# Expert tiles with the first half's activation transposes inside the second half's gate/up matmuls, ScalarE and VectorE in another order, and GpSimd computing 3 of 12 low parts

## The reference

```
for e in range(16):
    hid = silu(xt @ W_gate_e[e]) * (xt @ W_up_e[e])     # 1024 -> 512, twice
    y = y + combine[:, e:e+1] * (hid @ W_down_e[e])     # 512 -> 1024
```

## Time and profile before

| | |
|---|---|
| median of three runs | 1472.57 us |
| the profiled execution, span of its page | 1482.0 us |
| expert stage in it | 903 to 1414 us |
| PE busy over the span | 1236.9 us (83%) |
| DVE, ACT, POOL busy | 848.6, 639.1, 219.0 us |

### The profile page before, as it was taken

How to read it: one execution, slowest core, us unless ns; L and a number is a source line. 1 busy time by engine, 2 the same in 40 slices (tenths; PEclk the granted TensorE clock), 3 DMA queues, 4 the chain that set the end, 5 groups by cost and what they waited for, 6 DMA issues and landing times. The chain is left out here.

```text
span 1482.0 us, 24876 instructions
## 1 busy us (share of the span) xinstructions
PE 1236.9 (83%) x7835; PEld 1011.2 (68%) x7836; DVE 848.6 (57%) x1812; ACT 639.1 (43%) x1250; POOL 219.0 (15%) x307
## 2 busy tenths in 40 slices
PE   6479998999899999999589972999899989899910
PEld 1178876988697868887368752777677777777800
DVE  2623773367426762377445766587754575557339
ACT  4333453345434453345412214476543464446224
POOL 0200320022102220032000112011011101011132
PEclk9789998999899998999699985999899999999965
DMA  7513122221222122320453325889966596866156
GB/s 281 159 43 90 51 58 60 78 58 56 60 67 71 54 58 57 88 79 15 139 148 127 118 70 191 304 288 313 321 210 204 189 320 202 276 226 226 58 182 214
DMA packets 201385, 215.29 MB, mean 145 GB/s; under 512 B 15368, under 2 KB 166464, under 8 KB 201024
## 3 DMA queue, kind: packets, MB, share of 16 engines
q1 hardware_dynamic: 179136, 174.40, 37.1%
q0 software_dynamic: 10064, 34.42, 6.5%
q10 hardware_dynamic: 12112, 5.41, 1.3%
HBM read 187.40 MB, written 26.79 MB: 145 GB/s over the span
## 5 line engine op out<-in xcount | busy, mean ns | idle before, releaser
L703 PE MATMUL mixers_ps_proj<-early_h_hi,mixers_w_hi 128*128 128x352 f32 x384 | 129.5, 337 | 33.2 <-POOL mixers_a_hg L482 27.6
L1735 PE MATMUL experts_ps_g<-experts_w_hi,experts_x_hi 128*128 128x512 f32 x384 | 150.7, 392 | 2.2 <-DVE experts_x_lo L1664 2.2
L1736 PE MATMUL experts_ps_g<-experts_w_lo,experts_x_hi 128*128 128x512 f32 x384 | 150.4, 392 | 0.0
L1737 PE MATMUL experts_ps_g<-experts_w_hi,experts_x_lo 128*128 128x512 f32 x384 | 150.3, 391 | 0.0
L495 POOL TENSOR_TENSOR mixers_k_lv<-mixers_decay,mixers_hk 128x1024 f32<-128x1024 f32 (+2 forms) x40 | 79.7, 1995 | 343.1 <-ACT mixers_decay L571 333.2
L1659 DVE TENSOR_TENSOR experts_w_lo<-all_raw,experts_w_hi 128x1024 fp32r<-128x1024 f32 x96 | 113.8, 1223 | 27.5 <-ACT experts_w_hi L1608 24.5
L729 PE MATMUL mixers_ps_proj<-mixers_w_hi,early_h_hi 128*128 128x512 f32 (+1 forms) x288 | 119.8, 416 | 9.9 <-DVE mixers_w_lo L851 9.9
L704 PE MATMUL mixers_ps_proj<-early_h_lo,mixers_w_hi 128*128 128x352 f32 x384 | 127.3, 332 | 0.0
L705 PE MATMUL mixers_ps_proj<-early_h_hi,mixers_w_lo 128*128 128x352 f32 x384 | 127.2, 331 | 0.0
L1659 DVE TENSOR_TENSOR experts_w_lo<-experts_raw_more,experts_w_hi 128x1024 fp32r<-128x1024 f32 x96 | 111.8, 1221 | 14.4 <-ACT experts_w_hi L1608 13.1
L731 PE MATMUL mixers_ps_proj<-mixers_w_hi,early_h_lo 128*128 128x512 f32 (+1 forms) x288 | 114.0, 396 | 0.0
(11 more groups left out here) (269 smaller groups left out, 2710.9 us busy)
## 6 DMA issues: line engine op xcount, KB each, us to landing
experts_raw_more<-in_W_down_e_dram SPq DMA_DIRECT2D x128, 256.0 KB, 5.1
all_raw<-in_W_gate_e_dram SPq DMA_DIRECT2D x96, 256.0 KB, 5.7
all_raw<-in_W_up_e_dram SPq DMA_DIRECT2D x96, 256.0 KB, 6.7
all_raw<-in_W_in_dram SPq DMA_DIRECT2D x32, 512.0 KB, 4.2
all_raw<-in_W_ada_dram SPq DMA_DIRECT2D x32, 512.0 KB, 4.0
y_scratch<-experts_y POOLq DMA_DIRECT2D x24, 512.0 KB, 4.4
condition_w_ada_in<-in_W_ada_dram SPq DMA_DIRECT2D x4, 2048.0 KB, 8.2
experts_raw_more<-in_W_gate_e_dram SPq DMA_DIRECT2D x32, 256.0 KB, 3.5
```

The source lines that it names most:

```text
L703: pe.matmul(out, whi, xhi, start=(k == 0), stop=False)
L1735: pe.matmul(out, x_hi[:, k, :], w_hi[:, c, at], start=(k == 0), stop=False)
L1736: pe.matmul(out, x_hi[:, k, :], w_lo[:, c, at], start=False, stop=False)
L1737: ins = pe.matmul(out, x_lo[:, k, :], w_hi[:, c, at], start=False, stop=(k == KD - 1))
```

## The change

TensorE issues `turn_h(0)` in the middle of the second half's gate/up, after chunk 5, and `turn_h(1)` after the first quarter of the down projection. ScalarE and VectorE work on the turned hidden activation and on the chunks in an order to match. The low parts of chunks 2, 6 and 10 are computed by GpSimd in place of VectorE, with a semaphore of their own; in a tile that carries a split GpSimd does chunks 2 and 6 before its gather, and chunk 10 between the gather and the store of `y`.

```diff
+POOL_CHUNKS = (2, 6, 10)
@@ sync
-                    sp.wait_ge(lo_done, sp.snap(x * CH + (c + 1 - CH)))
+                    sp.wait_ge(*lo_count(sp, sp.snap(x - 1), c))
@@ gpsimd
+            def split(x, c, first):
+                pool.wait_ge(hi_done, c + 1 if first else pool.snap(x * CH + (c + 1)))
+                if not first:
+                    carry(pool, idle)
+                pool.tensor_tensor(w_lo[:, c], raw[c], f32(w_hi[:, c]), ALU.subtract).then_inc(pool_lo, 1)
+
+            for c in POOL_CHUNKS:
+                split(0, c, True)
+
             def tile(x, t, j, last, last_expert):
+                splits = last and not last_expert
+                following = pool.snap(x + 1) if splits else None
+                if splits:
+                    split(following, POOL_CHUNKS[0], False)
+                    split(following, POOL_CHUNKS[1], False)
                 start = pool.value_load(s.plan[0:1, bass.ds(x, 1)], min_val=0, max_val=SLOTS)
...
                 pool.wait_ge(xt_done, pool.snap(t + 1))
                 carry(pool, idle)
                 gather(column, pool.snap(t + 2))
+                if splits:
+                    split(following, POOL_CHUNKS[2], False)
                 pool.wait_ge(y_stored, pool.snap(t * 16 + 16))
@@ scalar (vector alike: product, h_low and x_low; its split skips POOL_CHUNKS)
                 some(0, 3)
                 silu(0)
-                some(3, 6)
+                some(3, 5)
+                h_high(0)
+                some(5, 7)
                 silu(1)
-                h_high(0)
+                h_high(1)
                 x_high(t)
-                h_high(1)
-                some(6, 9)
+                some(7, 11)
                 act.wait_ge(used, act.snap(t * CH + CH))
                 act.wait_ge(y_stored, act.snap(t * 16 + 16))
                 act.activation(y[:, 0:512], ps_y[0][:, :], ACT.Copy).then_inc(y0_done, 1)
-                some(9, CH)
+                some(11, CH)
@@ tensor
                         c = 4 * half + k // 2
+                        if half == 1 and k == 4:
+                            turn_h(0)
...
-                turn_h(0)
                 turn_x(t)
-                turn_h(1)
                 pe.wait_ge(y0_done, pe.snap(t + PRIMED))
                 pe.wait_ge(y1_done, pe.snap(t + PRIMED))
                 for f in range(KF):
+                    if f == 1:
+                        turn_h(1)
```

More of the change, by code:

```diff
@@ L1520, in phase_experts @@
         lists_in, index_done = sem("lists_in"), sem("index_done")
-        hi_done, lo_done, used = sem("hi_done"), sem("lo_done"), sem("used")
+        hi_done, used = sem("hi_done"), sem("used")
+        dve_lo, pool_lo = sem("dve_lo_done"), sem("pool_lo_done")
         x_in, xt_done, xhi_done, xlo_done = sem("x_in"), sem("xt_done"), sem("xhi_done"), sem("xlo_done")
@@ L1528, in phase_experts, with lo_count @@
         ident = s.const("ident")
+        def lo_count(e, x, c):
+            by_pool = c in POOL_CHUNKS
+            n = len(POOL_CHUNKS) if by_pool else CH - len(POOL_CHUNKS)
+            nth = 1 + sum((k in POOL_CHUNKS) == by_pool for k in range(c))
+            at = x * n + nth if isinstance(x, int) else e.snap(x * n + nth)
+            return (pool_lo if by_pool else dve_lo), at
         def experts(e, tile):
@@ L1657, in split @@
             def split(x, c, first):
+                if c in POOL_CHUNKS:
+                    return
                 dve.wait_ge(hi_done, c + 1 if first else dve.snap(x * CH + (c + 1)))
-                dve.tensor_tensor(w_lo[:, c], raw[c], f32(w_hi[:, c]), ALU.subtract).then_inc(lo_done, 1)
+                dve.tensor_tensor(w_lo[:, c], raw[c], f32(w_hi[:, c]), ALU.subtract).then_inc(dve_lo, 1)
             def x_low(t):
@@ L1689, in tile @@
                 product(0)
-                some(3, 6)
+                some(3, 5)
+                h_low(0)
+                some(5, 7)
                 product(1)
-                h_low(0)
+                h_low(1)
                 x_low(t)
-                h_low(1)
-                some(6, 9)
+                some(7, 11)
                 dve.wait_ge(used, dve.snap(t * CH + CH))
@@ L1724, in tile, with turn_h @@
                 t2 = pe.snap(t * 2 + PRIMED)
-                chunk0 = pe.snap(x * CH) if not isinstance(x, int) else x * CH
                 pe.wait_ge(xlo_done, pe.snap(t + 1))
                 pe.wait_ge(hid_done, t2)
+                def turn_h(n):
+                    pe.wait_ge(hid_done, pe.snap(t2 + (n + 1)))
+                    pe.wait_ge(hlo_done, t2)
+                    for f in range(2):
+                        ins = pe.transpose(ps_h[n][:, f, :], hid[:, (2 * n + f) * P:(2 * n + f + 1) * P], ident)
+                    ins.then_inc(ht_done, 1)
                 for half in range(2):
@@ L1739, in tile @@
                             ins.then_inc(used, 1)
-                def turn_h(n):
-                    pe.wait_ge(hid_done, pe.snap(t2 + (n + 1)))
-                    pe.wait_ge(hlo_done, t2)
-                    for f in range(2):
-                        ins = pe.transpose(ps_h[n][:, f, :], hid[:, (2 * n + f) * P:(2 * n + f + 1) * P], ident)
-                    ins.then_inc(ht_done, 1)
-                turn_h(0)
                 turn_x(t)
-                turn_h(1)
                 pe.wait_ge(y0_done, pe.snap(t + PRIMED))
```

4 lines of the change are left out of this document (2 added, 2 removed).

## The result

| | median of runs | range | ratio to before, 95% interval |
|---|---|---|---|
| before | 1471.73 us | 1469.38 to 1473.05 (4 runs) | |
| changed kernel | 1637.03 us | 1632.14 to 1639.94 (4 runs) | 1.111 [1.107, 1.1151] |

The changed kernel is slower by 165 us. The forecast was 1622 us, with 1560 to 1690 around it. The profiled execution of the changed kernel has a span of 1630.5 us. For before there are two profiled executions: that of the rows ahead of the prediction (1482.0 us) and a second one, taken later (1467.1 us, at a time of 1468.78 us). Where they differ I give both.

A forecast was written before the change was run, and what follows sets the result against it. The prediction took the late gather, queued on GpSimd, as what TensorE waits for. Terms 47.6 (singles) + 77 (closing tiles) + 13 (tile 0) + 12 (extras) = 149.6 us on the 1472.57 median gave 1622 us, range 1560 to 1690.

The forecast's parts named there:

- The mechanism: GpSimd's queue: gather held behind chunk 6's low part, issued at T0+15.6 in place of T0+4.7; split tiles take 29.6 us.
- The closing tiles: Seven closing tiles carrying a split: each grows from 18.6 to 29.6 us by the late gather, +77 us.
- The singles: Seven singles after tile 0: each grows from 22.8 to 29.6 us by the late gather, +47.6 us.
- tile 0: First tile of the stage, 21.8 us before: gather about 5 us later than in the template, +13 us.
- The extras: Eight extras: store of y and gather 2.4 us later, thinner traffic against it; +1.5 each, 12 us (bounds -1, +4 each).
- The signs: Traces expected: turn_x waits some 9 us in 15 tiles, late gather, idle weight queue, y store at T0+4, clock near 0.5.
- The longer chain: Split tiles: same held gather with every step at its upper bound, 34.7 us a tile, +248 us, 1720; chance 0.08.
- the shorter: Split tiles: same held gather with every step at its lower bound, 24.9 us a tile, +56 us, 1529; chance 0.08.
- Blocking without a held gather: 15 tiles: VectorE and GpSimd only block each other, up to 2.4 us each, at most 36 us, 1509; chance 0.02.
- The faster rival: GpSimd's waits for chunks 2 and 6 met by T0+1.8, only TensorE's saved waits remain: about -5 us, 1467; chance 0.01.
- The rule of the Trainium skill: VectorE two-SBUF-input and GpSimd SBUF-reading instructions exclude each other, up to 2.4 us per chunk; sum said to be unchanged.

The follow-up runs named there:

- Experiment 4: Changed kernel with all 12 low parts on VectorE; GpSimd only waits for chunk 6's high part ahead of the gather, no arithmetic: 1626.6 us, against 1508.73 without the wait.
- experiment 1: Changed kernel with GpSimd's plan load and gather moved ahead of all three of its low parts: 1478.2 us, ratio 1.0043.
- Experiment 9: Changed kernel with chunk 2's low part given back to VectorE; chunks 6 and 10 stay on GpSimd where they stand: 1621.05 us, ratio 1.0989.
- experiment 2: Changed kernel with all 12 low parts back on VectorE, keeping the new places of turn_h and the new engine order: 1508.73 us, ratio 1.0256.
- experiment 3: Changed kernel with GpSimd's chunks 2, 4, 10 in place of 2, 6, 10: 1612.85 us, ratio 1.0953.

## Why the prediction was right, step by step

**The mechanism** was named and holds. Experiment 4 shows the wait by itself, experiment 1 takes it away. The steps of a tile that carries a split (us after T0):

| | forecast | closing tile at 1202.61 | single at 1281.86 |
|---|---|---|---|
| high part of chunk 6 ends | 11.3 | 11.0 | 12.7 |
| low part of chunk 6 ends | 13.7 | 13.8 | 15.6 |
| gather issued | 15.6 | 14.8 | 16.6 |
| `turn_x` starts | 20.6 | 20.9 | 23.9 |
| next gate/up starts | 29.6 | 29.2 | 32.1 |

For the closing tiles each step is within 1 us. Two errors cancel: the gather was issued 0.8 us sooner than forecast, because plan and index cost 1.0 us behind the low part and not 1.9, and it landed in 6.1 us and not in 5.0. The estimate of 5.0 took the queues as empty from T0+13.8 on; the loads issued until T0+14.9 were still in flight (DMA share 0.84 over the wait).

**The singles** were mis-sized, by 2.5 us each. Their mean: gather issued at T0+16.7 and not 15.6, landing 6.7 us and not 5.0, 8.7 us behind `turn_x` and not 9.0. The landing is the largest of the three, and the closing tiles have it too (6.3 us). The late issue is the singles' own, and a step of the mechanism failed there: the prediction costed VectorE's slower subtractions at nothing, since "VectorE is not waited for". In the single at 1281.86, VectorE, GpSimd and TensorE in this order:

```profile
1286.64 4.57 DVE L1689 TENSOR_TENSOR experts_w_lo<-all_raw,experts_w_hi 128x1024 fp32r<-128x1024 f32 x2
1291.13 0.41 DVE L1710 TENSOR_TENSOR experts_hid<-experts_act_g,experts_ps_g 128x256 f32<-128x256 f32 x1
```

```profile
1287.38 2.73 POOL L1595 TENSOR_TENSOR experts_w_lo<-all_raw,experts_w_hi 128x1024 fp32r<-128x1024 f32 x1 [1.23 <-ACT experts_w_hi L1635]
```

```profile
1291.59 0.44 PE L1763 MATMUL experts_ps_h<-all_consts_sb,experts_hid 128*128 128x128 f32 x2 [1.41 <-DVE experts_hid L1710]
...
1305.75 1.97 PE L1749 MATMUL experts_ps_x<-all_consts_sb,experts_x_rows 128*128 128x128 f32 x8 [10.94 <-DMA experts_x_rows<-h_scratch,experts_index]
```

GpSimd's chunk 2 blocks two subtractions of VectorE, 4.57 us for two. The first product comes late, and `turn_h(0)`, which the change moved into the middle of gate/up, waits 1.41 us for it. That delays `h_high(0)` on ScalarE, chunks 5 and 6 behind it and so the gather: T0+16.6 in place of 14.8. The move made the product a thing that TensorE waits for, and the prediction still used the waits of before. Experiment 9 takes chunk 2 away: the gather of a single goes out at T0+15.6 on average, 1.1 us earlier, and the 7 singles are 8 us shorter together, about half of the 7 x 2.5 = 17.5 that were missed. It still goes out 1.1 us later than in a closing tile of that kernel (T0+14.5), and the landing stays (6.6 us); why this gather took 7.3 us to land, and singles more than closing tiles, was not tried apart.

**The closing tiles** (+81 or +82.5 against 77) and **tile 0** (+16.4 or +17.6 against 13) were right within their bounds.

**The extras** (20.3 or 19.8 us before, 19.0 after) have the wrong sign: -10.9 or -6.3 us against +12, outside the bound of -1 each only by the first profile. The store came out at T0+4.1 as forecast (T0+4.2). But the gather followed it after 2.93 us (1235.93 to 1238.86, above) and not after the 4.64 us that the same place took before (1256.83 to 1261.47, for which the store and the index copy stand in the earlier trace rows). The gather is thus only 0.6 us later in its tile (T0+7.0 against T0+6.4), where the prediction had 2.4. It had also read the place before too late: in the first tile of an expert the gather follows its store 1.7 us later than in a closing tile (4.64 us against 2.93), not some 3 us, since its index copy takes 0.18 us and that of the closing tile 1.02. Its flight was shorter, and TensorE's wait with it, 1.34 us where the first profile of before has 2.73. Windows over the two flights, of after and of before:

```profile
1238.86:1245.00 6.14, 4.80 (x25) 3.69 (x24) 0.84 (x2) 0.77 (x2) 0.99 (x1) 1.00 0.77 306
```

```profile
1261.48:1268.00 6.52, 4.81 (x23) 3.74 (x21) 6.44 (x7) 3.88 (x7) 0.97 (x1) 1.00 1.03 380
```

The thinner traffic that the prediction set against the later store seems to have been worth more than it: over all extras the landing takes 5.3 us on average, against 6.6 and 6.4 in the two profiles of before. No run holds the issue fixed and changes the traffic alone.

**The sum.** Forecast 149.6 us, measured 165 on the medians, 148.5 on the first profile and 163.4 on the second. That the first comes within 1 us is luck: singles, closing tiles and tile 0 are 25 us too low together, the extras 23 too high. The 15 us between forecast and measurement on the medians are two offsets, 9.4 and 6.5 us, less that 1 us. The first profile lies 9.4 us above the median that I put the sum on; the excess lies in its expert stage and raised the lengths of before from which I subtracted. And the changed kernel's profiled execution, its fastest of four, has a span 6.5 us below its median time.

**The signs.** The wait at `turn_x`, the gather's place, the queue of the weight loads and the store of `y` came as named. Two were off: the mean granted clock over the wait is 0.65 and not near 0.5, and the median landing 6.1 us and not 5.

**The rivals.** The longer chain (1720) and the shorter (1529) are excluded by the steps above. (Against the shorter the prediction also set a fall of the clock in waits of 3 us and less; its rows show one after 3.43 us.) Blocking without a held gather (1509) is excluded by the gather's place; its price was not nil, though: by experiment 9 it made 10 us of waits of `turn_h`. The faster rival would have needed the high part of chunk 6 by T0+1.8; it ended at T0+11.0. The rule of the Trainium skill that was weighed, "SBUF — State Buffer", section "Who interferes with whom", agrees with the rows (4.57 and 4.50 us for two subtractions that take 2.35 alone). What the prediction made of it, that the sum would be the same by it, was wrong by experiment 9.

**What stays open.** In the first tile of an expert the index copy starts 2.2 to 3.3 us after the end of the store of `y` in the first profile of before, where the store had to wait for its inputs, and 1.0 to 1.8 us after it in the changed kernel, where the store followed a low part with nothing to wait for. From store to gather that is 4.4 to 4.9 us against 2.5 to 3.4. In experiment 2, where the store had waited too, the index copy starts 3.27 us after it although VectorE runs one subtraction only in that time, so blocking by VectorE does not explain it. That the sequencer gets ahead while the engine computes fits these rows, but nothing here tests it.

## What to carry to other kernels

Before a wait goes onto an in-order queue, look at what stands behind it: here one semaphore wait ahead of a gather cost 118 us, and the kernel with all 48 subtractions behind the gather stood 4 us above the kernel before. "The engine is not waited for" is true only of the order in which it was measured. A move that makes its result due earlier, or a late link behind it (VectorE's copy, then the store, then the gather), turns it into the bound, so follow each chain across all engines to its end. Where a queue holds an urgent transfer behind a late one, try to give one of them to another engine, then look for the wait that it had covered: that gave 20 us, and moving VectorE's product ahead of one subtraction 16 more.

## What was not expected of the hardware

- VectorE and GpSimd, two-input operations on 128x1024 floats. GpSimd takes 2.40 us where VectorE has nothing under way at its start; in the stage the median of `experts_raw_more` chunks is 2.77 and the longest 3.11. VectorE's mean over the stage rises from 1223 ns before to 1525 and 1593 ns. The page's groups of after (busy time in us, mean ns of one, then the idle time ahead and its releaser):

```profile
L1595 POOL TENSOR_TENSOR experts_w_lo<-experts_raw_more,experts_w_hi 128x1024 fp32r<-128x1024 f32 x32 | 87.1, 2723 | 305.9 <-ACT experts_w_hi L1635 305.9
...
L1689 DVE TENSOR_TENSOR experts_w_lo<-all_raw,experts_w_hi 128x1024 fp32r<-128x1024 f32 x80 | 120.0, 1525 | 22.7 <-ACT experts_w_hi L1635 21.8
...
L1689 DVE TENSOR_TENSOR experts_w_lo<-experts_raw_more,experts_w_hi 128x1024 fp32r<-128x1024 f32 x64 | 99.2, 1593 | 5.9 <-ACT experts_w_hi L1635 3.7
```

- An idle TensorE of 9.6 us is paid twice: the work behind it ran at a mean granted clock of 0.79 and took 8.3 us in place of 6.8.
- A gather of 128 rows lands after 4.2 us at the least, near the end of the stage, and after up to 8.5 in traffic, so an earlier issue is worth only what the traffic at that time leaves: in the closing tiles of experiment 3 it went out 1.6 us earlier, and `turn_x` started 0.3 us earlier (T0+20.8 against 21.1).
